# Two-level weight products on TensorE: high-part products first, the low-part wait behind them

## What is computed

```python
p = h @ w_in[l]                                                # first block, 1024 x 4608
x = x + g2 * conv_ffn(h2, w_up[l], ffn_dw[l], ffn_dw_b[l], w_down[l])
...
h = h + jnp.square(jax.nn.relu(u @ w_ff1[l])) @ w_ff2[l]       # second block
```

## Time and profile before

| what | value |
|---|---|
| median of three executions | 1970.48 us |
| profiled execution | 1969.42 us, of which the profile's span is 1967.6 us |
| TensorE matmul (PE) busy | 1907.8 us, 97% of the span, 12494 instructions |
| TensorE weight load (PEld) busy | 1645.4 us, 84% |
| VectorE (DVE) | 1063.0 us, 54% |
| ScalarE (ACT) | 889.2 us, 45% |
| GpSimd (POOL) | 1184.9 us, 60%, of which 1166.9 us in L782 |
| TensorE clock granted | full (2.4 GHz) in 0.994 of the span |

### The profile page before, as it was taken

How to read it: one execution, slowest core, us unless ns; L and a number is a source line. 1 busy time by engine, 2 the same in 40 slices (tenths; PEclk the granted TensorE clock), 3 DMA queues, 4 the chain that set the end, 5 groups by cost and what they waited for, 6 DMA issues and landing times.

```text
span 1967.6 us, 34019 instructions
## 1 busy us (share of the span) xinstructions
PE 1907.8 (97%) x12494; PEld 1645.4 (84%) x12494; DVE 1063.0 (54%) x1988; ACT 889.2 (45%) x1517; POOL 1184.9 (60%) x904
## 2 busy tenths in 40 slices
PE   7999999999999999999899999999999999999997
PEld 5677677888888887877889999787899998779997
DVE  4899865354443324887647743876542048554402
ACT  3223444243433324525546644556554355555533
POOL 2444233424645554645569987674788876649895
PEclk9999999999999999999999999999999999999999
DMA  9942233628433343436465575532465564326663
GB/s 386 349 128 85 54 97 106 231 80 172 139 117 97 118 150 127 144 98 204 147 201 180 181 238 164 163 108 88 131 185 178 179 202 134 108 83 197 184 191 108
DMA packets 121977, 306.57 MB, mean 156 GB/s; under 512 B 29689, under 2 KB 52601, under 8 KB 121477
## 3 DMA queue, kind: packets, MB, share of 16 engines
q1 hardware_dynamic: 119096, 300.16, 48.0%
q10 hardware_dynamic: 2764, 4.80, 1.5%
HBM read 300.19 MB, written 8.06 MB: 157 GB/s over the span
## 4 chain that ended last, share of the span: by engine, by line
issue 37%; POOL 32%; PE 27%; DVE 2%; ACT 1%; POOLq 0%; ACTq 0%; DVEq 0%
POOL w_lo L782 32%; PE bank L1326 8%; PE bank L1328 8%; PE bank L1327 8%; PE bank L1898 1%; PE bank L1899 1%; PE bank L1900 1%; DVE nb L2153 1%; PE bank L2079 0%; ACT w_hi L825 0%; DVE v_lo L2153 0%; PE bank L1928 0%; POOLq L776 0%; ACT p L1221 0%; DVE rinv L2145 0%
## 5 line engine op out<-in xcount | busy, mean ns | idle before, releaser
L782 POOL TENSOR_TENSOR w_lo<-raw,w_hi 128x512 fp32r<-128x512 f32 x884 | 1166.9, 1348 | 764.1 <-ACT w_hi L825 762.1
L825 ACT ACTIVATE w_hi<-raw 128x1024 fp32r<-128x1024 f32 x442 | 465.9, 1056 | 291.9 <-PE bank L1328 210.6
L1326 PE MATMUL bank<-h_hi,w_hi 128*128 128x256 f32 (+1 forms) x1248 | 427.1, 342 | 3.9 <-POOL w_lo L782 1.9
L1327 PE MATMUL bank<-h_lo,w_hi 128*128 128x256 f32 (+1 forms) x1248 | 418.6, 335 | 0.0
L1328 PE MATMUL bank<-h_hi,w_lo 128*128 128x256 f32 (+1 forms) x1248 | 418.5, 335 | 0.0
L1326 PEld LDWEIGHTS bank<-h_hi,w_hi 128*128 128x128 f32 x1248 | 237.2, 190 | 45.6 <-issue 12.4
L1328 PEld LDWEIGHTS bank<-h_hi,w_lo 128*128 128x128 f32 x1248 | 237.1, 190 | 24.8
L1327 PEld LDWEIGHTS bank<-h_lo,w_hi 128*128 128x128 f32 x1248 | 237.4, 190 | 23.3 <-issue 0.2
L1326 PE MATMUL bank<-u_hi,w_hi 128*128 128x272 f32 (+1 forms) x736 | 211.8, 288 | 0.3 <-DVE u_lo L2153 0.3
L1328 PE MATMUL bank<-u_hi,w_lo 128*128 128x272 f32 (+1 forms) x736 | 210.2, 286 | 0.0
L1327 PE MATMUL bank<-u_lo,w_hi 128*128 128x272 f32 (+1 forms) x736 | 208.5, 283 | 0.0
(11 more groups left out here) (381 smaller groups left out, 3643.0 us busy)
## 6 DMA issues: line engine op xcount, KB each, us to landing
raw<-in_wstream SPq DMA_DIRECT2D x442, 512.0 KB, 3.6
ada_raw<-in_wada SPq DMA_DIRECT2D x48, 512.0 KB, 12.7
late_a<-in_wada SPq DMA_DIRECT2D x16, 512.0 KB, 5.0
late_b<-in_wada SPq DMA_DIRECT2D x16, 512.0 KB, 4.5
biash<-rpb_by_offset SPq DMA_DIRECT2D x64, 64.0 KB, 2.7
gates<-in_wada SPq DMA_DIRECT2D x8, 512.0 KB, 5.3
rpb_by_offset<-in_rpb SPq DMA_DIRECT2D x16, 224.0 KB
bias_by_distance<-vec ACTq DMA_DIRECT2D x1, 3264.0 KB
```

Of the source, the lines that this page charges most:

```text
L782: i = pool.tensor_tensor(lo[:, part, s, :], whole[:, part, :], hi[:, part, s, :].bitcast(F32), ALU.subtract)
L825: act.activation(w_hi[q >= first["l2", 0]][:, :, s, :], raw[:, s, :].rearrange("p (g c) -> p g c", c=PAIR), ACT.Copy)\
L1326: pe.matmul(o, hi, a_hi, start=start, stop=False)
L1327: pe.matmul(o, hi, a_lo, start=False, stop=False)
```

## The change

`three` is split into `two` (the products with the high weights) and `third` (the one with the low weights). Six callers (`chunk`, `up`, `down`, `down_kept`, `ff1`, `ff2`) now wait for `w_hi_ready`, make all 16 high-weight products of the slab, then wait for `w_lo_ready`, and make the 8 low-weight products. The others keep `three` and `weights` ahead of it. That is 360 of the 442 slabs. The core of it:

```diff
+            def high_weights(i, it=None):
+
+                pe.wait_ge(sem("w_hi_ready"), i + 1 + (0 if it is None else it * 8))
+
+            def two(o, i, k, a_hi, a_lo, start):
+
+                pe.matmul(o, tile(w_hi, i, k), a_hi, start=start, stop=False)
+                pe.matmul(o, tile(w_hi, i, k), a_lo, start=False, stop=False)
+
+            def third(o, i, k, a_hi, stop):
+
+                return pe.matmul(o, tile(w_lo, i, k), a_hi, start=False, stop=stop)
 ...
             def chunk(i, b, T, a_hi, a_lo, key, reader, h_key=None, t0=0):
 
-                weights(i)
+                high_weights(i)
                 claim(b)
                 for k in range(DC):
                     if h_key:
                         pe.wait_ge(*after("norm_lo", (h_key, k)))
-                    mm = three(bank[b][:, t0:T], i, k, a_hi[:, k, t0:T], a_lo[:, k, t0:T], k == 0, k == DC - 1)
+                    two(bank[b][:, t0:T], i, k, a_hi[:, k, t0:T], a_lo[:, k, t0:T], k == 0)
+                weights(i)
+                for k in range(DC):
+                    mm = third(bank[b][:, t0:T], i, k, a_hi[:, k, t0:T], k == DC - 1)
                 mm.then_inc(*done("slab_used", i))
 ...
                 def ff1(j, b, it=None):
                     plus = 0 if it is None else it * 8
-                    weights(s + j, it)
+                    high_weights(s + j, it)
 ...
                     for k in range(DC):
                         if j == 0:
                             pe.wait_ge(*after("norm_lo", ((layer, 4), k)))
-                        mm = three(lin[b % 4][:, cols], s + j, k, ffn_in[layer][0][:, k, cols], ffn_in[layer][1][:, k, cols], k == 0, k == DC - 1)
+                        two(lin[b % 4][:, cols], s + j, k, ffn_in[layer][0][:, k, cols], ffn_in[layer][1][:, k, cols], k == 0)
+                    weights(s + j, it)
+                    for k in range(DC):
+                        mm = third(lin[b % 4][:, cols], s + j, k, ffn_in[layer][0][:, k, cols], k == DC - 1)
                     mm.then_inc(*done("slab_used", s + j))
 ...
                     for a, m in enumerate(ms):
                         for b, j in enumerate(js):
-                            mm = three(bank[m][:, cols], s + n, b + 4 * a, f2_hi[:, j, cols], f2_lo[:, j, cols], j == 0, j == FF2_C - 1)
+                            two(bank[m][:, cols], s + n, b + 4 * a, f2_hi[:, j, cols], f2_lo[:, j, cols], j == 0)
+                    weights(s + n)
+                    for a, m in enumerate(ms):
+                        for b, j in enumerate(js):
+                            mm = third(bank[m][:, cols], s + n, b + 4 * a, f2_hi[:, j, cols], j == FF2_C - 1)
                         if j == FF2_C - 1 and m < ms[-1]:
                             mm.then_inc(*done("ff2_sum", (layer, m)))
```

More of the change, by code:

```diff
@@ L1319, in weights, with tile, three @@
                 pe.wait_ge(sem("w_lo_ready"), i + 1 + (0 if it is None else it * 8))
-            def three(o, i, k, a_hi, a_lo, start, stop, col=None):
+            def high_weights(i, it=None):
+                pe.wait_ge(sem("w_hi_ready"), i + 1 + (0 if it is None else it * 8))
+            def tile(w, i, k):
                 n = i >= first["l2", 0]
                 g, h = (k % 4, k // 4) if n else (k // 2, k % 2)
-                hi, lo = (w[n][:, g, i % RING, h * P:(h + 1) * P] for w in (w_hi, w_lo))
-                pe.matmul(o, hi, a_hi, start=start, stop=False)
-                pe.matmul(o, hi, a_lo, start=False, stop=False)
-                return pe.matmul(o, lo, a_hi, start=False, stop=stop)
+                return w[n][:, g, i % RING, h * P:(h + 1) * P]
+            def two(o, i, k, a_hi, a_lo, start):
[3 more added lines that the diff above has]
+                return pe.matmul(o, tile(w_lo, i, k), a_hi, start=False, stop=stop)
+            def three(o, i, k, a_hi, a_lo, start, stop):
+                two(o, i, k, a_hi, a_lo, start)
+                return third(o, i, k, a_hi, stop)
             def chunk(i, b, T, a_hi, a_lo, key, reader, h_key=None, t0=0):
-                weights(i)
+                high_weights(i)
                 claim(b)
@@ L1695, in up @@
                         i = s + 2 * j + w
-                        weights(i, it)
+                        high_weights(i, it)
                         bk = (2 * b + w) % 4
@@ L1703, in up @@
                         for k in range(DC):
-                            mm = three(bank[bk][:, 0:T], i, k, h_hi[:, k, 0:T], h_lo[:, k, 0:T], k == 0, k == DC - 1)
+                            two(bank[bk][:, 0:T], i, k, h_hi[:, k, 0:T], h_lo[:, k, 0:T], k == 0)
+                        weights(i, it)
+                        for k in range(DC):
+                            mm = third(bank[bk][:, 0:T], i, k, h_hi[:, k, 0:T], k == DC - 1)
                         mm.then_inc(*done("slab_used", i))
@@ L1725, in down @@
                             claim(m)
-                        mm = three(bank[m][:, 0:T], s + j, m, dn_hi[:, j % 2, 0:T], dn_lo[:, j % 2, 0:T],
-                                   j == 0, j == FF_C - 1)
-                        if j == FF_C - 1 and m < DC - 1:
-                            mm.then_inc(*done("down_sum", (layer, m)))
+                        two(bank[m][:, 0:T], s + j, m, dn_hi[:, j % 2, 0:T], dn_lo[:, j % 2, 0:T], j == 0)
+                    weights(s + j, it)
+                    for m in ms:
+                        mm = third(bank[m][:, 0:T], s + j, m, dn_hi[:, j % 2, 0:T], False)
                     return mm
@@ L1748, in down_kept @@
                     js, ms = DOWN_ORDER[n]
-                    weights(s + n)
+                    high_weights(s + n)
                     if js[0] == 0:
@@ L1754, in down_kept @@
                         for b, j in enumerate(js):
-                            mm = three(bank[m][:, 0:SEQ], s + n, b * len(ms) + a, fa_hi[:, j, :], fa_lo[:, j, :], j == 0, j == DOWN_LAST)
+                            two(bank[m][:, 0:SEQ], s + n, b * len(ms) + a, fa_hi[:, j, :], fa_lo[:, j, :], j == 0)
+                    weights(s + n)
+                    for a, m in enumerate(ms):
+                        for b, j in enumerate(js):
+                            mm = third(bank[m][:, 0:SEQ], s + n, b * len(ms) + a, fa_hi[:, j, :], j == DOWN_LAST)
                         if j == DOWN_LAST and m < ms[-1]:
```

3 lines of the change are left out of this document (added).

## The result

The changed kernel takes 1972.80 us (median of 18 executions, 1970.02 to 1976.61), the kernel before 1969.72 us beside it (18 executions, 1966.08 to 1972.34). The ratio is 1.0020, with a 95% interval of 1.0013 to 1.0027: 3.1 us slower where 2.0 us faster was forecast. Measured side by side the two kernels can be told apart to 0.07%, finer than the 0.2% that the prediction allowed. The profiled execution took 1972.47 us, its span is 1970.6 us at a mean clock of 0.993.

The account below looks back on a forecast made before the run. TensorE, busy 97% of the span, was taken as the bound. Terms -4.7 + 0.87 + 0.83 + 0.3 + 1.7 - 1.0 = -2.0 us took 1970.48 to 1968.5 us; range 1963.5 to 1973.

Parts of the forecast that it names:

- the fourth down slab: Layer 1 down loop: TensorE's stop for the slab's low part at 1159.5 goes away, gain 1.7 us.
- the steps with 272 columns: Second block, layer 0: no sign could be told for the change in product steps; 0, between -1 and +1 us.
- the first `ff1` slabs: Second block: seven more products stand behind the last activation, costing 0.87 us in layer 0 and 0.83 in layer 1.
- the last chunk: Last ff2 slab: the even chunk ends 8 products later, delaying VectorE's adds and the serial tail; cost 0.3 us.
- the second wait: Split slabs: 360 more waits, hidden by TensorE's queue, costed at nothing.
- the steps of `ff1` and `ff2` in layer 1: Second block: more steps to a new k cost 21 ns a slab; 1.7 us on 83 slabs including 19 front ones.
- An earlier TensorE makes it earlier too: Glu slab of layer 1: the 1.1 us wait is gained, as VectorE in the following attention waits for TensorE.
- the front slabs: Second block, both layers: low-part waits at front slabs go away, gain 0.7 + 3 x 0.3 = 1.6 us.
- rival 3: Attention of either block: VectorE's chain sets the time, the 1.1 and 1.6 are given back, 1971.2 us; chance 0.12.
- TensorE waits for both: Layer 0 up slabs at 490 and 497: up_g and the low part both hold the start; gain only 0.3 us.
- the explanation by the position of the tiles: TensorE's products: step length depends on where loaded weights lie against streamed activations; steps closing a 64-byte gap are slower.
- With the stop gone it may stay at 113: Layer 1 down slabs: the step may stay at 113 ns instead of 118; bounds 0 and 2.0, taken as 1.0 us gain.

Follow-up runs that it names:

- experiment 3: Changed kernel with the first ff1 slab of each layer back in the old, unsplit order: 1971.39 us, ratio 1.0010 to the kernel before.
- experiment 2: Kernel before with only ff2 and ff1 split, except the first ff1 slab of each layer: 1972.17 us, ratio 1.0015.
- experiment 5: Kernel before with only chunk split, in both blocks: 1970.02 us, ratio 1.0000.
- 7: Changed kernel with VectorE's v_lo<-nb,v_hi operation written as scalar_tensor_tensor: 1973.19 us, ratio 1.0020 to the kernel before.
- 12: Kernel before with up, down and down_kept split, no pause on GpSimd: 1967.83 us, ratio 0.9991.
- experiment 9: Changed kernel with GpSimd waiting for VectorE's v_lo<-nb,v_hi ahead of its last first-block slab: 1972.99 us, ratio 1.0020 to the kernel before.
- 1: Kernel before with only down_kept split (22 slabs of layer 1): 1968.57 us, ratio 0.9993.
- 8: Changed kernel with VectorE's v_lo<-nb,v_hi as six operations of one row each: 1975.08 us, ratio 1.0023 to the kernel before.
- 10: Kernel before with up, down and down_kept split, plus a pause in GpSimd's row: 1966.02 us, ratio 0.9985.
- 11: Changed kernel with ff1 and ff2 as before, plus a pause in GpSimd's row: 1967.39 us, ratio 0.9992 to the kernel before.
- experiment 4: Kernel before, unsplit, with only the tile order changed in ff1 (j > 0) and ff2: 1971.23 us, ratio 1.0012.
- 6: Kernel before with only up (both layers) and down (layer 0) split: 1967.67 us, ratio 0.9992.

## Why the prediction was wrong

The direction came out wrong: 3.1 us slower, not 2.0 us faster. The 1972.8 us lie just inside the upper end of the stated range, and the terms below show that this is no credit to the sum. The step that failed first was to count a wait that goes away as time gained. The 1.1 us of glu and the 0.7 + 0.3 us of layer 0's front slabs, like the 0.6 us of layer 1's, were won and were given back in full within 20 us, because VectorE, by way of ScalarE, set the time there. Beside it, three terms were mis-sized: the fourth down slab, the steps with 272 columns, and the up slabs.

Right in kind and size were: the first `ff1` slabs (0.87 and 0.83 forecast, 0.85 and 0.83 measured), the last chunk (0.3; 0.21), the second wait (0; 0), the low-slab waits that go, `PE <- POOL w_lo` from 7.2 to 2.6 us (forecast: about 3), and the steps of `ff1` and `ff2` in layer 1 (64 slabs at 21 ns, 1.3 us; 0.60 + 0.64 in experiment 3's and the changed kernel's steady slabs, 2.84 to 2.86; the two loops of experiment 2 cost 1.7).

Wrong were these:

- **"An earlier TensorE makes it earlier too"** (glu, 1.1 us), and the same step, unsaid, for the front slabs (1.6 us). The step that failed outright. VectorE has no idle time there. In glu the gain came and was given back 12 us later, 1.17 against 1.22. In the front loops of layer 0 the two waits gave 1.2 us, and the wait ahead of the `pj` products grew from 2.02 to 3.09 us: 23.81 us before, 23.80 after. In layer 1 the front loops take the same time, too (176.70 and 176.78 us up to the first `ff1` slab). It was rival 3, in both blocks, at a chance of 0.12, and experiment 5 shows it alone. Its condition, that VectorE is idle there only 1 to 3 us at a time, was the right one to look at. The question that I left out was what bounds the stretch behind the wait, and VectorE's rows say it.
- **The fourth down slab (1.7 us).** The gain is there, 1.9 us, but I followed it no further than the end of its slab. The 40 us of GpSimd's pace behind it were not examined: it makes a slab in 2.50 us where TensorE takes 2.72, so it catches up only slowly. The stop had spared VectorE a meeting with GpSimd's row. The first front slab takes 14.67 to 14.83 us in the five kernels with the stop. Without it, it takes 16.2 us (the changed kernel, 7 and 12) where the clock was at half for the same 3.4 us, so 1.4 us are given back. The pause of experiment 9 brings that to 15.43. In the five others without the stop (1, 3, 8, 10 and 11, the last two with the pause) the clock was at half for 6.8 us there, and the slab takes 16.6 to 18.1. No kernel with the stop has that, so the longer idle time may cost some clock as well; that is not shown.
- **"TensorE waits for both"** (the up slabs, 0.3 us). Mis-sized, in the other direction: 1.78 us. I took two operations that end together for two conditions of one start, without reading for which slab the wait on `up_conv` asks. This is the largest gain of the change that was kept.
- **The steps with 272 columns (0, between -1 and +1).** 0.75 + 0.39 = 1.1 us, at the edge of the bound. The rows gave no sign to choose, and zero was a choice: the one thing that I had argued, that low products behind each other step slower with 256 columns, spoke for a cost. The front loops of layer 0 add 0.2 us. Also the explanation by the position of the tiles did not survive experiment 4; why the new order is slower stays open.
- **"With the stop gone it may stay at 113" (-1.0 us).** The down slabs do take 2.72 us in the changed kernel. But experiments 4 and 6 have the stop (4.53 and 4.55 us) and take 2.72 us as well, while the kernel before and experiment 5 take 2.83, and experiment 2 changes from one to the other. So the short step does not need the change, and what it gave in this comparison (1.4 us of the loop's 3.3) is no gain to count on. That the stop plays a part is not excluded: all nine kernels without it step at 2.72 (but for one slab with a short wait), of the five with it only two do.
- **Not in the prediction: a stretch at the lower clock.** The changed kernel has one in the gate loop of layer 1, 946.60 to 950.01, that the kernel before does not have. Windows, changed kernel:

```profile
940.00:945.00 5.00, 4.05 (x35) 3.85 (x33) 4.66 (x11) 3.59 (x7) 5.00 (x5) 1.00 0.27 80
945.00:950.00 5.00, 4.17 (x15) 3.39 (x16) 1.40 (x3) 1.19 (x2) 2.56 (x2) 0.66 0.88 305
```

The granted clock is 0.66 in that window, 1.2 GHz for two thirds of it and 2.4 for the rest, behind two waits of 1.03 and 0.75 us for VectorE that the kernel before has as well. The loop is 1.69 us longer. It stands in six of the nine traces with a split `up` and in none of the other five, so it is likelier in the changed kernel, at some 1.1 us on average, but one trace a kernel does not settle that. (The table of the time before says that the clock was full in 0.994 of the span. That is the mean granted clock: in that trace it was at half for 22 us, 1.1% of the span, so such stretches stand in the kernel before as well, elsewhere.)

Sum by stages: up -1.8, glu and qk 0, the stop with what is given back -0.4, the waits of the front loops 0 and their longer steps +0.2, the steps in `ff1` and `ff2` +2.4, their first slabs +1.7, the tail +0.2, half clock +1.1: +3.4 us. The medians of experiments 1, 2, 5 and 6, each against its own kernel before, are -0.2, +3.4, +0.4 and -2.0, 1.6 together; these four leave out only the first slabs of `ff1` (1.7), so they give +3.3. Both stand beside +3.1 measured. The agreement is better than the half clock term and the scatter of the medians warrant.

## What to carry to other kernels

A wait that you remove is worth what the next engine's slack behind it is worth: before counting it, look at whether the engine that feeds the next stretch (here VectorE ahead of the attention, GpSimd ahead of the second block) has idle time there. Splitting a loop pays only in the loops that wait; in those that don't it still changes the order of the products, and on an engine that is busy 97% of the time 0.4 to 0.8% more a step in the four `ff` loops (2.4 us) outweighed all waits that were kept (2.2 us). And when two operations end just ahead of a start, read the counts of its waits in the code before calling either a cause.

## What the runs showed of the hardware

- A VectorE operation with two inputs in SBUF can be held through a whole row of GpSimd's pieces: 11.8 us over nine of them, whatever its form or size (experiments 7 and 8), and 1.88 us with a pause in the row. Elsewhere it gets in behind one piece: `u_lo` at 1772.85 in the changed kernel took 1.62 us instead of the 0.49 of its sister at 1770.02. The Trainium skill, SBUF — State Buffer, section "SBUF: two separate sides", says that the two engines share a port pair under an exclusive lock that is held for a whole instruction. The short cases agree (a piece takes 1.25 to 1.35 us). The 11.8 us go beyond it, and why GpSimd goes first nine times in a row there was not found.
- The same `down_kept` stream runs at 113 or at 118 ns a product, in different executions of kernels that are the same up to there. In experiment 2 it changes in the middle, behind a slab of 3.26 us: 2.83 us a slab ahead of it, 2.72 behind.
- The order of equal products changes TensorE's pace by 0.5 to 0.8%, with every input ready (643 products in 80 us become 640 and 638, 594 in 70 us become 590).
- Stretches of TensorE at half clock stand in other places in each kernel's trace: 19 to 38 us in all, of a span of 1964 to 1975 us. A comparison of single traces has to set them aside stage by stage.
